# A chain of accumulating GpSimd DMAs added to a two-layer decoder trunk

## The reference

```
for layer in range(DEPTH):
    if layer % N_MIXERS == 0:
        h = h + fox_mixer(rmsnorm(h, fox_norm[j]), ...)
    else:
        h = h + retention_mixer(rmsnorm(h, ret_norm[j]), ...)
    h = h + sqrelu_mlp(rmsnorm(h, mlp_norm[layer]), mlp_up[layer], mlp_down[layer])
return rmsnorm(h, final_norm)
```

## Time and profile before

| | |
|---|---|
| median of two runs | 2603.8 us |
| span of the profiled execution | 2602.8 us |
| TensorE busy | 2583.9 us (99%) |
| VectorE busy | 1396.4 us (54%) |
| ScalarE busy | 1194.6 us (46%) |
| GpSimd busy | 36.7 us (1%) |
| moved by the 16 DMA engines | 483.41 MB, 186 GB/s in the mean |
| moved by the queue that GpSimd's DMAs use | 7.87 MB |
| mean granted TensorE clock | 0.999 |

### The profile page before, as it was taken

How to read it: one execution, slowest core, us unless ns; L and a number is a source line. 1 busy time by engine, 2 the same in 40 slices (tenths; PEclk the granted TensorE clock), 3 DMA queues, 4 the chain that set the end, 5 groups by cost and what they waited for, 6 DMA issues and landing times.

```text
span 2602.8 us, 34966 instructions
## 1 busy us (share of the span) xinstructions
PE 2583.9 (99%) x11770; PEld 2136.2 (82%) x11770; DVE 1396.4 (54%) x1565; ACT 1194.6 (46%) x1446; POOL 36.7 (1%) x43
## 2 busy tenths in 40 slices
PE   8999999999999999999999999999999999999998
PEld 6888888888888888888888888888888888888887
DVE  5545455555555555565555555555555455555554
ACT  6445444444434434455455344445444344443443
POOL 0000000000000000000000000000000000000000
PEclk9999999999999999999999999999999999999999
DMA  6545456555555555565555655555555555555554
GB/s 231 175 140 170 153 194 203 181 192 181 188 194 180 186 193 190 194 210 176 180 188 194 199 189 175 175 194 183 177 197 188 192 185 187 192 193 193 194 186 137
DMA packets 132851, 483.41 MB, mean 186 GB/s; under 512 B 15025, under 2 KB 15297, under 8 KB 132033
## 3 DMA queue, kind: packets, MB, share of 16 engines
q1 hardware_dynamic: 131040, 474.81, 54.6%
q0 software_dynamic: 1760, 7.87, 0.9%
HBM read 480.53 MB, written 2.10 MB: 185 GB/s over the span
## 4 chain that ended last, share of the span: by engine, by line
PE 99%; ACT 0%; DMA 0%; DVE 0%; SPq 0%; issue 0%; ACTq 0%; DVEq 0%
PE acc L353 31%; PE acc L355 31%; PE acc L354 31%; PE tr L371 2%; DMA raw<-in_w_stream 0%; PE sc L455 0%; PE sc L592 0%; PE sc L454 0%; PE sc L453 0%; PE mix L607 0%; PE mix L605 0%; PE mix L606 0%; PE mix L463 0%; ACT w_hi L654 0%; PE sc L416 0%; PE tr L479 0%
## 5 line engine op out<-in xcount | busy, mean ns | idle before, releaser
L924 DVE TENSOR_TENSOR w_lo<-raw,w_hi 128x1024 fp32r<-128x1024 f32 x896 | 1076.0, 1223 | 443.1 <-ACT w_hi L654 414.5
L654 ACT ACTIVATE w_hi<-raw 128x1024 fp32r<-128x1024 f32 x896 | 931.6, 1058 | 603.8 <-PE acc L355 340.0
L353 PE MATMUL acc<-w_hi,xT_hi 128*128 128x512 f32 x2176 | 864.0, 397 | 3.9 <-DVE w_lo L924 3.2
L355 PE MATMUL acc<-w_hi,xT_lo 128*128 128x512 f32 x2176 | 848.9, 390 | 0.0
L354 PE MATMUL acc<-w_lo,xT_hi 128*128 128x512 f32 x2176 | 847.4, 389 | 0.0
L353 PE MATMUL acc<-w_hi,aT_hi 128*128 128x512 f32 x1408 | 550.9, 391 | 0.1
L355 PE MATMUL acc<-w_hi,aT_lo 128*128 128x512 f32 x1408 | 548.1, 389 | 0.0
L354 PE MATMUL acc<-w_lo,aT_hi 128*128 128x512 f32 x1408 | 547.7, 389 | 0.0
L355 PEld LDWEIGHTS acc<-w_hi,xT_lo 128*128 128x128 f32 x2176 | 408.8, 188 | 87.1
L353 PEld LDWEIGHTS acc<-w_hi,xT_hi 128*128 128x128 f32 x2176 | 409.1, 188 | 86.0 <-issue 3.8
L354 PEld LDWEIGHTS acc<-w_lo,xT_hi 128*128 128x128 f32 x2176 | 409.5, 188 | 80.8
(11 more groups left out here) (134 smaller groups left out, 600.9 us busy)
## 6 DMA issues: line engine op xcount, KB each, us to landing
raw<-in_w_stream SPq DMA_DIRECT2D x896, 512.0 KB, 4.4
gain<-in_gains POOLq DMA_DIRECT2D x4, 1024.0 KB, 6.7
scratch<-in_gn POOLq DMA_DIRECT2D x8, 256.0 KB, 5.4
scratch<-in_decay POOLq DMA_DIRECT2D x8, 192.0 KB, 3.3
h<-in_x SPq DMA_DIRECT2D x4, 256.0 KB, 5.2
h<-in_x SPq DMA_DIRECT2D x1, 1024.0 KB, 11.0
out<-raw SPq DMA_DIRECT2D x1, 1024.0 KB, 3.9
out<-raw SPq DMA_DIRECT2D x4, 256.0 KB, 2.5
```

The source lines that it names most:

```text
L353: pe.matmul(acc[tok][:, :], hi_t[:, x_cols], w_hi[:, w_cols], start=(kt == 0), stop=False)
L355: m = pe.matmul(acc[tok][:, :], lo_t[:, x_cols], w_hi[:, w_cols], start=False, stop=(kt == KT - 1))
L654: act.activation(w_hi[:, s * SW:(s + 1) * SW], raw[:, s % RAW * SW:(s % RAW + 1) * SW], ACT.Copy).then_inc(hi_made, 1)
L924: dve.tensor_tensor(w_lo[:, c], raw[:, s % RAW * SW:(s % RAW + 1) * SW], w_hi[:, c].bitcast(F32), ALU.subtract).then_inc(lo_made, 1)
```

## The change

GpSimd gets a tile `sums`, columns 4608 to 5119 of `scratch`, 128 x 512 float32 (256 KB). It first copies the first 512 columns of the stream's first slot there. Then, for each of the 32 blocks of the first MLP and for the slots 0, 2, 4 and 6 of it, it waits until `lo_made` has passed that slot and until the DMA before has landed, and issues a DMA that reads the first 512 columns of that slot from `w_stream` and adds them to `sums` (`accum_op=ALU.add`). That makes 128 adding DMAs and one copy. Each DMA adds 16 to `sum_in`. GpSimd waits for the last, and VectorE does in `rotated`, since `rot` lies over `sums`. Nothing reads the sums.

```diff
+SUMS = 4
...
+        sum_in = sem("sum_in")
+        sums = cut(4608, NB)
...
             load_gain(0)
             load_gain(1)
             load_gain(2)
+
+            pool.wait_ge(lo_made, FOX_BLOCKS * SLOTS + 1)
+            pool.dma_start(sums, w_stream[0, 0][:, 0:NB]).then_inc(sum_in, 16)
+            with pool.Fori(0, MLP_BLOCKS) as i:
+                for n in range(SUMS):
+                    s = n * (SLOTS // SUMS)
+                    pool.wait_ge(lo_made, i * SLOTS + (FOX_BLOCKS * SLOTS + s + 1))
+                    pool.wait_ge(sum_in, i * (SUMS * 16) + (n + 1) * 16)
+                    pool.dma_start(sums, w_stream[bass.ds(i + FOX_BLOCKS, 1), s, :, 0:NB]
+                                   .rearrange("o p n -> (o p) n"), accum_op=ALU.add).then_inc(sum_in, 16)
+            pool.wait_ge(sum_in, MLP_BLOCKS * SUMS * 16 + 16)
...
+                dve.wait_ge(sum_in, MLP_BLOCKS * SUMS * 16 + 16)
                 dve.tensor_tensor(r[0], e[:, :, 0, :], cos, ALU.mult)
```

## The result

The changed kernel takes 3155.2 us (median of two runs, 3154.5 to 3155.8) against 2603.8 us: a ratio of 1.212, with a 95% interval of 1.210 to 1.214. That is 551 us slower. The profiled execution has a span of 3152.8 us, 550.0 more than before. The forecast was 3244 us with a range of 3052 to 3564.

A forecast was written before the change was run, and what follows sets the result against it. TensorE, busy for 99% of the span, was taken as the bound. Profiled time 2602.8 + 640 (128 additions at 5.0) - 2.3 slack + 2.5 small terms = 3243 us, so 3244 for the runs' median; range 3052 to 3564 us.

The forecast's parts named there:

- The place: GpSimd's in-order stream: the additions stand behind `load_gain(2)`, so all 128 run after the first MLP, from about 1153 us.
- The wait: VectorE's `rotated` stands for the whole chain, stopping ScalarE, SyncE and TensorE's transposes; rotation moves by 640 us.
- The slack: Between VectorE's rotation end at 1154.95 and TensorE's transposes at 1157.21: 2.3 us that hide part of the chain.
- The price of one addition: P, per addition in GpSimd's chain: 0.7 + 3.0 + 1.3 = 5.0 us, between 3.3 and 7.8.
- the gap from landing to issue: First part of P, on GpSimd: from the semaphore to the start of the next issue, 0.7 us.
- issue to landing of a copy: Second part of P: a plain copy's time with the weight stream stopped, 3.0 us.
- the adding: Third part of P: reading the destination too, 1.3 us, twice the bare 0.65 us of a second read.
- The small terms: After the hole: 1.5 us for TensorE's half-pace matmuls, about 1 us for refilling ScalarE's and SyncE's pipelines.
- Adding is free: Rival on P: adding costs nothing and bookkeeping is shorter, P 3.1 us, time 3001 us; chance 0.06.
- adding is dear: Rival on P: DMA engines read, add and write each row without overlap, P 10 us, 3884 us; chance 0.08.
- The other side: Rival: GpSimd passes L300 before the first MLP, additions run beside it, not slower, 2604 us; chance 0.02.

The follow-up runs named there:

- e2: Changed kernel with the whole chain of additions moved ahead of `load_gain(2)`, behind `load_gain(1)`; 2631.3 us, ratio 1.010.
- e3: Changed kernel with the sums on columns 3840 to 4351 and VectorE's wait on `sum_in` in `rotated` removed; 3133.0 us, ratio 1.203.
- e1: Changed kernel with `accum_op=ALU.add` left out, so the 128 chained DMAs copy instead of adding; 3051.8 us, ratio 1.172.
- e9: Changed kernel with the additions started ahead of `load_gain(1)`, that load after four blocks and `load_gain(2)` after the other 28; 2625.9 us, ratio 1.009.
- e5: Changed kernel with each addition, and the first copy, taking 1024 columns (512 KB) instead of 512; 3345.6 us, one run.

## Why the prediction was right, and where it was off

**The place.** Right, and it was the step on which all hung: the additions started at 1154 us, behind `load_gain(2)`. e2, which moves the same lines ahead of that load, gave back 524 us.

**The wait.** Right as to the hole: it begins at the transposes of the staged tile, and VectorE, ScalarE and SyncE stand with it. The slack was given as 2.3 us and was: VectorE's rotation came 551.4 us later (1702.72 against 1152.72, and the 1.4 us of lead), and TensorE stood for 549.1. What the prediction left unsaid, and e3 showed, is that VectorE's new wait is not what makes the chain expensive: GpSimd's own next loads would have held VectorE 33 us later.

**The price of one addition.** This is the term that was mis-sized: 5.0 us, measured 4.29, and 128 x 0.71 is 91 us, against the 89 us by which 3244 was too high; the other terms, off by some 1 to 2 us each, nearly cancel. Of its three parts, the gap from landing to issue was 0.7 us and is 0.69; issue to landing of a copy was 3.0 and is 2.8 (e1); the adding was 1.3 and is 0.80. The least landing of the 192 KB table, 2.7 us, was a better guide than the 3.0. The doubling of the bare second read, "because reading, adding and writing have to follow one another", had no row behind it, and the runs do not bear it out: what adding put on the period is 0.80 us for 256 KB, nearer to the bare 0.65 than to 1.3, and 1.65 us for 512 KB, nearer to 1.3 than to 2.6.

The DMA engines' time for an addition is 2.0 to 2.4 times a copy's. That agrees, as to the factor of two, with the rule that the prediction cited from the Trainium skill, page "Collectives: The Full Stack", section "The bandwidth ceiling: the fold count and why AG ≠ RS ≠ AR", by which a reduction is slower than a copy only for its second read, and not for the adding. By it the prediction's sum would have been 3161 us, 6 above the measured time; part of that is luck, since it takes 0.65 us for the adding where 0.80 was measured, and the copy's 0.2 us too much made up for it. The rule speaks of a rate; the period rose here by 23% only, since most of it is latency.

The measured landings of copies, 2.2, 2.8 and 3.5 us for 64, 256 and 512 KB, also bear on a formula of the Trainium skill, page "DMA: Bandwidth & Descriptors", section "Anatomy of one DMA — SWDGE (gpsimd) path": 2.0 us and the bytes over 436 GB/s. As an estimate from that page it gives 2.2, 2.6 and 3.2 us, so it is within 0.1 us for the small one and 0.2 and 0.3 us low for the others. The 0.7 us from a landing to the next issue come on top of it here.

**The small terms.** The slow matmuls after the hole were taken as 1.5 us and cost 2.3. The refilling of ScalarE's and SyncE's pipelines was taken as 1 us and cost nothing: TensorE has no wait for `w_lo` after the hole that it did not have before.

**The rivals.** "Adding is free" is ruled out by e1, "adding is dear" by the period. The other side, additions beside the MLP, was priced at 2604 us as long as one takes at most 5.6 us. The prediction had one P for both places, 5.0 us, and its landing time was chosen for a stretch in which the stream stands still. e2 and e9 show that the condition is not met: beside the stream an addition takes 5.8 us in the mean, and the time is 2626 to 2631 us. Had the lines stood ahead of `load_gain(2)`, the same P would have given 2604 us, 1% too low.

## What to carry to other kernels

A semaphore wait gives the earliest moment of an instruction; its place in the engine's stream can make it much later (here by some 700 us). Before pricing DMAs added to an idle engine, find the wait that stands ahead of them, and the loads that stand behind them. A chain in which each DMA waits for the one before pays latency each time (here 2.7 of 4.3 us); two tiles with a semaphore each nearly halved the period (2.21 us). And a DMA's price in a quiet stretch does not hold beside a stream: with the weight stream on 57% of the DMA engines' time, 4.3 us became 5.8.

## What the runs showed of the hardware

- An adding DMA issued by GpSimd has an issue instruction of 0.87 us, a copy one of 0.54 us, whether a row is 512 B, 2 KB or 4 KB long; with 32 rows instead of 128 they are 0.77 and 0.50 us.
- An adding DMA keeps the DMA engines busy for 2.0 to 2.4 times as long as a copy of the same bytes, and the page of the profile counts the bytes once (41.70 MB for GpSimd's queue in the changed kernel and in e1 alike; the HBM side of both is a read of 256 KB per DMA).
- It is also cut differently. By the packets of GpSimd's queue, less the 1760 of before, an adding DMA of 128 rows made 144 packets with 64, 256 and 512 KB alike, and one of 32 rows made 48; a copy made 32, 80 and 144, and 32 with 32 rows. That is one packet per row plus 16 for the adding and one per 4 KB plus 16 for the copying. The engines' time is 2.0 times a copy's where the packets are as many (512 KB) and 2.4 times where they are 144 against 32 (64 KB in 128 rows), but 2.0 times again at 48 against 32 (64 KB in 32 rows). That the finer cut makes this difference is likely by these numbers, and not shown. The queue's line of the page (packets, MB, share of the engines' time), in e1 and in e5; that of the changed kernel stands above:

```profile
q0 software_dynamic: 12080, 41.70, 3.9%
```

```profile
q0 software_dynamic: 20336, 75.52, 12.4%
```

- Three of the 128 waits in the changed kernel are not put down to a landing but marked as issue, 12.9 us in all against 3.4 us for a usual one. That is 0.02 us of the mean period; its cause was not looked into.
- Additions beside the stream, at 5.8 us each, made the stream's slots land in 5.0 us instead of 4.4, and that hardly reached TensorE: in e2 it had no wait in the first MLP, in e9 two, of 0.9 us (at 522 us, 11 us after the 1 MB gain load was issued beside the chain) and of 0.6 us (at 1102 us).
